# The even mixer's moving sums on VectorE, over zero-padded buffers, in place of GpSimd

## What is computed

```python
POOL_WINDOWS = (2, 4, 8, 16)                  # one group of 128 channels each
cs = jnp.cumsum(ug, axis=1)
for g, w in enumerate(POOL_WINDOWS):
    c = cs[:, :, g]
    lagged = jnp.pad(c, ((0, 0), (w, 0), (0, 0)))[:, :s]
    count = jnp.minimum(pos + 1, w)
    means.append((c - lagged) / count)
diff = jnp.stack(means, axis=2) - ug
y = jnp.einsum('bsgc,gcd->bsgd', diff, pool_w).reshape(b, s, POOL_WIDTH)
return y * pool_scale
```

## Time and profile before

| what | us |
|---|---|
| three runs | 1211.92, 1210.61, 1210.66 |
| median | 1210.66 |
| the profiled execution's own time | 1211.39 |
| its span in the trace | 1210.1 |
| PE busy | 1195.6 |
| DVE busy | 891.9 |
| ACT busy | 649.0 |
| POOL busy | 59.9 |

### The profile page before, as it was taken

How to read it: one execution, slowest core, us unless ns; L and a number is a source line. 1 busy time by engine, 2 the same in 40 slices (tenths; PEclk the granted TensorE clock), 3 DMA queues, 4 the chain that set the end, 5 groups by cost and what they waited for, 6 DMA issues and landing times. The chain is left out here.

```text
span 1210.1 us, 16639 instructions
## 1 busy us (share of the span) xinstructions
PE 1195.6 (99%) x6678; PEld 1029.6 (85%) x6678; DVE 891.9 (74%) x1221; ACT 649.0 (54%) x830; POOL 59.9 (5%) x80
## 2 busy tenths in 40 slices
PE   9999999999999999999999999999999999999997
PEld 8888888888887888888898888888888987888886
DVE  6977989837776798874688787776467568777744
ACT  6545666635566666653585645444327674544430
POOL 0000000000000000000006310000012001000000
PEclk9999999999999999999999999999999999999999
DMA  9755455564533465565524557555527432755530
GB/s 355 248 204 191 171 178 198 188 221 167 187 119 134 179 196 182 179 217 200 178 78 141 167 212 246 186 197 191 177 90 261 140 139 96 253 199 183 188 125 35
DMA packets 32510, 217.81 MB, mean 180 GB/s; under 512 B 3745, under 2 KB 4017, under 8 KB 7857
## 3 DMA queue, kind: packets, MB, share of 16 engines
q1 hardware_dynamic: 30560, 210.39, 49.8%
q0 software_dynamic: 1728, 6.29, 1.6%
q10 hardware_dynamic: 144, 0.07, 0.0%
HBM read 215.67 MB, written 1.05 MB: 179 GB/s over the span
## 5 line engine op out<-in xcount | busy, mean ns | idle before, releaser
L942 PE MATMUL ps<-t,t 128*128 128x512 f32 (+3 forms) x2328 | 535.2, 386 | 0.0
L1503 DVE TENSOR_TENSOR t<-t,t 128x2048 fp32r<-128x2048 f32 (+3 forms) x200 | 448.0, 2252 | 95.3 <-PE ps L942 85.6
L942 PEld LDWEIGHTS ps<-t,t 128*128 128x128 f32 x2328 | 422.6, 188 | 80.4 <-issue 0.5
L1184 ACT CAST t<-t 128x2048 fp32r<-128x2048 f32 (+3 forms) x200 | 374.6, 1883 | 204.6 <-PE ps L942 102.8
L873 PE MATMUL ps<-t,t 128*128 128x512 f32 x1274 | 306.0, 390 | 0.3 <-DVE t L1624 0.3
L873 PEld LDWEIGHTS ps<-t,t 128*128 128x128 f32 x1274 | 238.7, 188 | 52.3 <-ACT t L1184 0.9
L879 PEld LDWEIGHTS ps<-t,t 128*128 128x128 f32 x1456 | 187.2, 191 | 7.5
L879 PE MATMUL ps<-t,t 128*128 128x256 f32 x1456 | 189.5, 283 | 0.0
L1577 DVE SCALAR_TENSOR_TENSOR t<-t,t,t 128x254 f32<-128x254 f32 (+1 forms) x176 | 73.2, 478 | 10.2 <-ACT t L1201 10.2
L1241 ACT CAST t<-t 128x512 fp32r<-128x512 f32 x44 | 27.3, 620 | 96.9 <-DVE t L1608 96.9
L1624 DVE TENSOR_REDUCE t<-ps 128x512 f32<-128x1024 f32 x40 | 48.9, 1223 | 41.0 <-PE ps L881 41.0
(11 more groups left out here) (210 smaller groups left out, 866.0 us busy)
## 6 DMA issues: line engine op xcount, KB each, us to landing
t<-in_wts SPq DMA_DIRECT2D x192, 1024.0 KB, 5.0
t<-in_rows POOLq DMA_DIRECT2D x12, 512.0 KB, 4.2
t<-in_wts SPq DMA_DIRECT2D x4, 528.0 KB, 4.1
t<-in_wts SPq DMA_DIRECT2D x2, 768.0 KB, 5.7
t<-in_wts SPq DMA_DIRECT2D x2, 592.0 KB, 4.1
t<-in_x_in SPq DMA_DIRECT2D x2, 512.0 KB, 4.1
t<-in_wts SPq DMA_DIRECT2D x2, 512.0 KB, 7.0
out<-t SPq DMA_DIRECT2D x4, 256.0 KB, 2.0
```

The source lines that it names most:

```text
L942: ins = mm(ps[:, t_bank(stage, t, j), 0:c1 - c0], a, w[:, k, c0:c1], start=kt == 0 and part == 0, stop=kt == KTS[stage] - 1 and part == 2)
L1184: copy(wh[:, k, 0:w], wraw[:, r, 0:w]).then_inc(s_hi, 1)
L1503: tt(wl[:, k, 0:w], wraw[:, r, 0:w], wh[:, h, 0:w].bitcast(F32), ALU.subtract).then_inc(s_lo, 1)
```

## The change

`pool_sums` on POOL goes away, and DVE gets `moving_sums`, called at the same step ahead of the same last instruction. Ahead of each of the four buffers stand 4 or 8 columns of zeros and ahead of each row of `us` one, cleared once by POOL at the step `pool_weights` (`clear_pads`, five memsets). An addition then runs over all 256 columns and the copies of the first columns are not needed. Each level is one addition that waits for the one before. The list of steps is the same.

```diff
@@ memory
-    us = area_at(area.at).take([128, 4, S])
+    us = area_at(area.at).take([128, 4, S + 1])
...
-    sums = [area_at(brow_at + 1024 * i).take([128, S]) for i in range(4)]
+    rows_area = area_at(brow_at)
+    pads = (8, 4, 8, 4)
+    sums = [rows_area.take([128, n + S]) for n in pads[:3]]
     yo = area.take([128, 2, 256])
+    sums.append(area.take([128, pads[3] + S]))
...
+    def summed(i, back=0):
+        return sums[i][:, pads[i] - back:pads[i] - back + S]
@@ ACT, step us
-                copy(us[:, 2 * k[0]:2 * k[0] + 2, :].rearrange("p a b -> p (a b)"),
-                     ps[:, f_bank("even", 7 + k[0]), :]).then_inc(s_us, 1)
+                copy(us[:, 2 * k[0]:2 * k[0] + 2, 1:S + 1],
+                     ps[:, f_bank("even", 7 + k[0]), :].rearrange("p (a b) -> p a b", a=2)).then_inc(s_us, 1)
@@ DVE
+        def moving_sums(g):
+            at = 2 * (g % 2)
+            dve.wait_ge(s_us, g // 2 + 1)
+            dve.wait_ge(s_pads, 5)
+            dve.wait_ge(s_in, 32)
+            if g >= 2:
+                dve.wait_ge(s_mix, g - 1)
+            dve.own(tt(summed(at), us[:, g, 1:S + 1], us[:, g, 0:S], ALU.add))
+            for i in range(1, g + 1):
+                dve.settle()
+                dve.own(tt(summed(at + i % 2), summed(at + (i + 1) % 2), summed(at + (i + 1) % 2, 1 << i), ALU.add))
+            cnt = cs[:, CST["cnt"] + 16 * g:CST["cnt"] + 16 * g + 16]
+            src, dst = (summed(at + (g + n) % 2) for n in range(2))
+            dve.settle()
+            dve.own(tt(dst[:, 0:16], src[:, 0:16], cnt, ALU.mult))
+            dve.settle()
+            tt(dst[:, 0:16], dst[:, 0:16], us[:, g, 1:17], ALU.subtract).then_inc(s_psum, 1)
...
             elif name == "sum":
                 g = k[0]
+                moving_sums(g)
                 dve.wait_ge(s_psum, g + 1)
@@ POOL
-        def pool_sums(g):
...
-            for i in range(g + 1):
-                sh, dst = 1 << i, bufs[i % 2]
-                if i:
-                    pool.settle()
-                copy(dst[:, 0:sh], src[:, 0:sh])
-                pool.own(tt(dst[:, sh:S], src[:, sh:S], src[:, 0:S - sh], ALU.add))
-                src = dst
...
+        def clear_pads():
+            pool.wait_ge(*x_ready(4, 7))
+            memset(us[:, :, 0:1], 0.0).then_inc(s_pads, 1)
+            for i in range(4):
+                memset(sums[i][:, 0:pads[i]], 0.0).then_inc(s_pads, 1)
...
-            elif kind == "sum":
-                pool_sums(k[0])
+            elif kind == "pool_weights":
+                clear_pads()
```

More of the change, by code:

```diff
@@ L480, in program @@
     Ph = area.take([128, 4, S], F32R)
-    us = area_at(area.at).take([128, 4, S])
+    us = area_at(area.at).take([128, 4, S + 1])
     Pl = area.take([128, 4, S], F32R)
+    area.at += 32
     xtok, xdt = (area.take([128, 2, D]) for _ in range(2))
@@ L549, in program @@
     s_ah, s_dready, s_psum = sem("s_a"), sem("s_decay_logs"), sem("s_pool_summed")
+    s_pads = sem("s_pool_pads_cleared")
     s_pdiff, s_mix, s_ph, s_pl = sem("s_pool_diff"), sem("s_pool_mixed"), sem("s_pool_hi"), sem("s_pool_lo")
@@ L1031, in even_step @@
                 pe.wait_ge(s_pdiff, g + 1)
-                mm(ps[:, bank, 0:S], pwt[:, g, :], sums[2 * (g % 2) + (g + 1) % 2][:], start=True,
+                mm(ps[:, bank, 0:S], pwt[:, g, :], summed(2 * (g % 2) + (g + 1) % 2), start=True,
                    stop=True).then_inc(s_mix, 1)
@@ L1732, in even_step @@
                 g = k[0]
-                src, dst = sums[2 * (g % 2) + g % 2], sums[2 * (g % 2) + (g + 1) % 2]
+                src, dst = (summed(2 * (g % 2) + (g + n) % 2) for n in range(2))
+                moving_sums(g)
                 dve.wait_ge(s_psum, g + 1)
-                stt(out=dst[:, 16:S], in0=src[:, 16:S], scalar=1.0 / (2 << g), in1=us[:, g, 16:S], op0=ALU.mult,
+                stt(out=dst[:, 16:S], in0=src[:, 16:S], scalar=1.0 / (2 << g), in1=us[:, g, 17:S + 1], op0=ALU.mult,
                     op1=ALU.subtract).then_inc(s_pdiff, 1)
```

## The result

| | us |
|---|---|
| kernel before, median of 8 | 1210.95 |
| changed kernel, median of 8 | 1213.94 |
| ratio, 95% interval | 1.0022 (1.0013 to 1.0032) |
| changed kernel, lowest and highest | 1211.75 and 1215.20 |
| profiled execution, time and span | 1214.09 and 1212.8 |

The kernel has become slower by 0.22%, 3.0 us in the medians, where 1.08 had been forecast. The measured median lies above the forecast range, which ended at 1213.2. The executions also lie further apart: 3.5 us instead of the 1.3 of the kernel before in this series, though on one of the later chips the kernel before spreads over 2.7 us as well (1210.50 to 1213.20 in 25 executions). So the profile of one execution has to be read together with the list of all.

The account below looks back on a forecast made before the run. PE was taken to bound the kernel, with DVE's last difference setting `mix3`. Sums on DVE cost 2.55 us, 1.47 come back, so 1.08 added to the median of 1210.66 gives 1211.7 us; range 1210.3 to 1213.2.

Parts of the forecast that it names:

- What bounds the kernel, and who waits for whom: Whole kernel: PE bounds it, busy 1195.6 of 1210.1 us; POOL's sums delay DVE, whose last difference sets `mix3`.
- The cost of the additions: DVE's four sums: 0.45 us per addition, 0.22 per small instruction, giving 0.89, 1.34, 1.79 and 2.24 us, together 6.26.
- What comes back from GpSimd: DVE instructions lengthened beside POOL's moving-sum additions become short again, giving back 1.47 us.
- the four places named: DVE instructions at 654.40, 665.60, 668.40 and 671.36 us, long beside POOL's additions; expected gains 0.41, 0.42, 0.42 and 0.22 us.
- The sum: At DVE's last difference before `mix3`: 2.55 us later, less 1.47 given back, so 1.08 us later.
- The stalls: PE's waits: at an earlier decay matmul 1.2 us in place of 1.5, and at `mix3` about 2.1 us.
- The step that failed: From the `mix3` wait of about 2.1 us to kernel time: 1.08 us added to the median, giving 1211.7.
- the rivals: Three alternatives: long DVE instructions not POOL's doing (0.08), DVE done before PE needs it (0.05), effects cancelling (0.15).
- The range: Kernel time of 1210.3 to 1213.2 us, taking in the cancelling case and most of rival (a).
- rival (a): Long DVE instructions aren't POOL's doing, nothing comes back: last difference 2.66 us late, slower by 0.22%; chance 0.08.

Follow-up runs that it names:

- both: Changed kernel with sums kept on VectorE, plus GpSimd additions of the old kind that nobody reads; median 1216.68 us, 3.6 above the changed kernel.
- layout: Changed kernel with the sums back on GpSimd, new padded buffers and memsets kept; median 1211.12 us beside 1211.30 of the kernel before.
- again3: Changed kernel unaltered, one more execution, profiled to look for a fall of the clock; 1214.65 us.
- again: Changed kernel unaltered, measured a second time in 11 executions; median 1213.07 us, ratio 1.0011 against the kernel before.

## Why the prediction was wrong

- **What bounds the kernel, and who waits for whom.** Right. The last difference on VectorE sets `mix3` in the trace of the kernel before and in all four of the changed kernel.
- **The cost of the additions.** Right: 0.86, 1.32, 1.79 and 2.25 us against 0.89, 1.34, 1.79 and 2.24.
- **What comes back from GpSimd.** Right, 1.48 us in the four places named against 1.47; `both` shows the cause by putting GpSimd's additions back.
- **The sum.** Forecast 1.08 us for the stretch; 0.99 in three traces. The stalls were forecast at 1.2 and 2.1 and are 1.26 and 2.25. The fastest executions agree: 1211.41 against 1210.50 for the kernel before on one chip, 0.9 us, and 1211.47 against 1210.43 on the next, 1.0. So do the medians once the wait ahead of `mix3` is filled: 0.7 us (1211.86 against 1211.18) and 0.95 (1211.82 against 1210.87) above the kernel before on the same chip.
- **The step that failed** is the one from there to the time. I wrote that `mix3` "now waits about 2.1 us there", and gave that wait no price but its own length: the clock isn't among the rivals, although I had read a granted clock of 1.00 behind stalls of up to 1.53 us in one execution and took it for a property of the kernel. Of the 31 executions of the changed kernel 13 have a mean clock of 0.997 or below, and they took 1213.06 to 1215.20 (median 1214.19); the other 18 have a median of 1212.0, the trace with a fall of 1214.65 us among them. A fall behind `mix3` costs 1.6 us, in the one trace that shows it. In the medians of the two later series the changed kernel is 1.8 and 1.5 us above the kernel before on the same chip, 0.5 to 0.8 more than the 0.99 of the stretch. In the kernel before, 15 of 85 executions on the later chips have such a clock, and lie at a median of 1211.35 against 1210.90; where `layout`'s trace shows such a fall, the stall at `mix3` took most of it up.
- **The range** was made of terms of a sum, for one execution. It did not contain that executions of the same kernel differ, by the clock and by weight chunks that land up to 1 us later, which put most of 1.7 us into the first profile of after. The medians of the two later series, 1213.07 and 1212.63, do lie inside the range, but for a reason that it was not made of: it reached so high to take in rival (a).
- **Rival (a)** gives almost the measured ratio, 0.22%, and is false: all that it says would stay away came back. A number that fits is no evidence for its mechanism; had I read the ratio alone I would have taken it.

What stays open: the first series of the changed kernel (median 1213.94) is 0.9 us above the second and 1.3 above the third, and no run shows why. Of the 3.0 us measured there, 1.0 are the stretch, another 0.5 to 0.8 are in the later series too, where filling the wait ahead of `mix3` takes as much away (0.8), and the rest stays open. The first series has more low clocks, 5 of 8 executions against 8 of 22. Late chunks at the feed-forward heads are in two of the changed kernel's four traces at 0.4 to 0.9 us each, and in the one of the kernel before at 0.3. Of the nine traces with the sums on VectorE five have such a wait, of the five others one. That is too few to say whether the change has any part in how often they come. Nor does any run show why the clock falls in some executions behind a given stall and not in others.

## What to carry to other kernels

Price a wait on TensorE by more than its length: where a change lengthens one idle time and shortens another, look at what stands behind each, and whether anything there would absorb a stretch at half the clock (1.6 us here). Read several executions before believing a granted clock of 1.00 in one, and compare the fastest ones as well as the medians; the first give the mechanism, the second what it costs. Whether work is cheaper on another engine is settled by whose queue is full at that place: here ten additions were a third shorter on VectorE, took away 1.5 us of mutual delay on VectorE, and still cost 1 us.

## What the runs showed of the hardware

- TensorE's granted clock fell from 2.4 to 1.2 GHz for part of the next 5 to 15 us behind idle times of 1.53, 1.81, 2.00 and 2.26 us, in some executions and not in others with the same stall to 0.01 us (2.26 with a fall in `again3`, 2.25 without in `again`; 1.53 with in `layout`, 1.53 without in the kernel before).
- Matmuls that nobody reads, put into a wait, made a kernel faster in the median: 1211.86 against 1212.63 on the same chip, the lowest times being equal to 0.06 us.
- VectorE and GpSimd delay each other where they overlap, in float32: a VectorE addition of 256 columns took 0.79 us in place of 0.41 beside an addition on GpSimd (`both`), and a copy of two columns on GpSimd took 2.13 us beside a weight part of 2.4 us on VectorE (kernel before, at 662.41) and 0.26 elsewhere (`both`, at 668.34).
